# A deeper pipeline of attention jobs, a reordered second layer and whole-row norms in a three-part transformer kernel

## The reference

```python
def first_block(x, p, ...):                       # one layer
    proj = rmsnorm(x, attn_pre_g) @ w_in          # q, and keys and values of four kinds
    k_cmp, v_cmp = compress_kv(kc, ...), compress_kv(vc, ...)
    o_nsa = nsa_attention(q_n, k_cmp, v_cmp, ksl, vsl, kwn, vwn, gates, slopes)  # cmp + slc + win
    o_swa = swa_attention(q_s, k_s, v_s, sinks, slopes)                          # sliding, 128 wide
    x = x + rmsnorm(concat(o_nsa, o_swa) @ w_o, attn_post_g)
    y = gelu(causal_dwconv(a)) * u  @ w_down      # a, u = split(rmsnorm(x) @ w_gate_up)
    x = x + rmsnorm(y, mlp_post_g)
    return x + (p @ w_ple) * sigmoid(x @ w_ple_gate)

def hybrid_layer(x, ...):                         # twice, on 16 + 512 tokens
    q, k, v, gate_a, u_b, gate_b, q_idx, k_idx, w_idx, merge = split(rms_norm(x) @ w_in)
    # index scores choose for each query which keys it sees (the rest is masked), then attention
    y_a = (attention(rope(norm(q)), rope(norm(k)), v, chosen) * silu(gate_a)) @ w_a
    y_b = (multiscale_pool(u_b) * silu(gate_b)) @ w_b
    return x + (sigmoid(merge_a) * y_a + sigmoid(merge_b) * y_b) @ w_out
```

## Time and profile before

| | us |
|---|---|
| median of 3 runs | 1639.17 |
| lowest and highest | 1632.9 and 1644.02 |
| the profiled execution | 1644.22 |
| its span, first to last instruction | 1642.3 |
| PE busy in the span | 1547.3 |
| POOL, DVE, ACT busy | 972.7, 907.3, 542.9 |

### The profile page before, as it was taken

One profiled execution on the slowest core, in us unless ns is written; L12 is line 12 of the kernel. 1 busy time (PEld: TensorE's weight loads), 2 busy tenths in 40 slices (PEclk: granted clock), 3 DMA queues, 4 the chain that ended last, 5 costly groups with the idle time before them and its releaser, 6 DMA issues.

```text
span 1642.3 us, 26836 instructions
## 1 busy us (share of the span) xinstructions
PE 1547.3 (94%) x9758; PEld 1305.0 (79%) x9758; DVE 907.3 (55%) x2009; ACT 542.9 (33%) x1285; POOL 972.7 (59%) x1540
## 2 busy tenths in 40 slices
PE   6989878989999999998999999999999989899999
PEld 6766544757778777886899988889999977788999
DVE  4444555157667670017567778944446679684251
ACT  3244565233333320013365233341135523223210
POOL 5442400645655678778886655446888663255685
PEclk9999988989999999999999999999999998799999
DMA  6111000212223223332222212112222221111223
GB/s 234 52 52 39 27 1 1 65 51 90 89 89 102 90 89 103 97 95 65 85 76 78 78 52 65 52 52 72 91 91 77 74 70 41 38 63 55 72 94 106
DMA packets 37353, 119.59 MB, mean 73 GB/s; under 512 B 5376, under 2 KB 7552, under 8 KB 36992
## 3 DMA queue, kind: packets, MB, share of 16 engines
q1 hardware_dynamic: 35824, 115.74, 21.6%
q10 hardware_dynamic: 1424, 2.41, 0.4%
HBM read 116.02 MB, written 2.10 MB: 72 GB/s over the span
## 4 chain that ended last, share of the span: by engine, by line
PE 77%; DVE 12%; ACT 4%; issue 3%; POOL 3%; DMA 0%; ACTq 0%; POOLq 0%; SPq 0%; DVEq 0%
PE ps L682 62%; PE ps L701 2%; DVE score L2183 2%; PE ps L1123 2%; DVE score L2182 2%; PE ps L869 2%; POOL wlo L586 2%; PE ps L803 2%; PE ps L1199 1%; PE ps L695 1%; PE ps L714 1%; ACT pts L1399 1%; POOL whi L582 1%; DVE probs L2303 1%; DVE probs L2284 1%
## 5 line engine op out<-in xcount | busy, mean ns | idle before, releaser
L682 PE MATMUL ps<-hh,whi 128*128 128x512 f32 (+2 forms) x1736 | 572.0, 330 | 17.7 <-ACT merge L1643 6.2
L682 PE MATMUL ps<-hl,whi 128*128 128x512 f32 (+2 forms) x1736 | 560.9, 323 | 0.0
L682 PE MATMUL ps<-hh,wlo 128*128 128x512 f32 (+2 forms) x1736 | 559.8, 322 | 0.0
L582 POOL TENSOR_SCALAR whi<-raw 128x256 fp32r<-128x256 f32 x592 | 266.0, 475 | 380.2 <-PE ps L682 369.6
L586 POOL TENSOR_TENSOR wlo<-raw,whi 128x256 fp32r<-128x256 f32 x592 | 463.5, 813 | 12.3
L682 PEld LDWEIGHTS ps<-hh,whi 128*128 128x128 f32 x1736 | 331.0, 191 | 62.6 <-issue 20.2
L682 PEld LDWEIGHTS ps<-hh,wlo 128*128 128x128 f32 x1736 | 331.2, 191 | 25.4
L682 PEld LDWEIGHTS ps<-hl,whi 128*128 128x128 f32 x1736 | 331.0, 191 | 25.1 <-issue 2.0
L646 POOL TENSOR_TENSOR wlo<-raw,whi 128x256 fp32r<-128x256 f32 x160 | 134.8, 873 | 92.7 <-ACT whi L1442 92.7
L1791 DVE TENSOR_TENSOR tmp<-tmp 128x512 f32<-128x512 f32 x14 | 11.6, 826 | 134.7 <-ACT tmp L1481 101.1
L682 PE MATMUL ps<-plain_high,whi 128*128 128x264 f32 (+2 forms) x288 | 83.6, 290 | 1.9 <-POOL wlo L586 1.5
(11 more groups left out here) (315 smaller groups left out, 2721.2 us busy)
## 6 DMA issues: line engine op xcount, KB each, us to landing
raw<-in_w SPq DMA_DIRECT2D x200, 512.0 KB, 3.3
x<-in_x SPq DMA_DIRECT2D x4, 512.0 KB, 7.4
out<-x SPq DMA_DIRECT2D x8, 256.0 KB, 6.0
raw<-in_w SPq DMA_DIRECT2D x12, 128.0 KB, 2.6
raw<-in_w SPq DMA_DIRECT2D x4, 384.0 KB, 3.3
cw_k<-in_cw1k SPq DMA_DIRECT2D x1, 1024.0 KB, 5.5
cw_v<-in_cw1v SPq DMA_DIRECT2D x1, 1024.0 KB, 7.3
raw<-in_w SPq DMA_DIRECT2D x4, 256.0 KB, 2.9
```

The costliest lines, as they stand in the source:

```text
L582: ins = pool.tensor_scalar(whi[s][:, c:c + PIECE], raw[s][:, c:c + PIECE], 1.0, 0.0, ALU.mult, ALU.add)
L682: mm = pe.matmul(out, lhs, rhs, start=start and n == 0, stop=stop and n == 2)
```

## The change

- **Attention jobs.** Everything behind `biased` comes one round later: DVE does `weighted(i-2)`, PE transposes job i-3 and finishes job i-4, ACT copies job i-3 and puts only one exponential ahead of the copies. There are four buffers: the 8 sliding jobs share `probs` by halves of a row, the later ones use `third`, `probs` and the place of a weight tile that is no longer needed. A job waits for the transposes of the job four before it.
- **Fills.** `FIRST` has the window keys behind two query units of group 0, and `fills1` projects them in round 9 (from round 6). The queries of group 1 come in rounds 14 and 17 (from 10 and 13). SP's loads and POOL's splits follow `FIRST`.
- **"pre" norm.** DVE adds up the squares of the 8 chunks, and PE sums them in four matmuls at the end. ACT's first square waits for the transfer of `late` too.
- **Embedding.** `embed_out` 1 to 3 stand before ACT's loop, 4 to 7 in its first four rounds. The root of the tokens comes right behind `embed_out(0)`.
- **Start of both hybrid layers.** The inverse root is again a whole row of 528 on all partitions: 2 matmuls over the summed squares, a root on ACT, a reciprocal on DVE. The keys' norm waits for query unit 0 on PE, then takes 2 matmuls, a row-wide mean on DVE, root on ACT and reciprocal on DVE, and four multiplications. All of it stands ahead of the first rotation on DVE. The four sets of small matmuls (L737 twice, L1085, and the spreading of the keys' factor) and `keys_out` go.
- **Last layer's plan.** Two more merges are in the lead and the index scores of tile 2 stand closer together. All picks of tile 2 are at the end of DVE's lead, not in slots 0 and 1. Side work of tile 3 is in slots 0 to 4 (from 2 to 5), of tile 4 in slots 5 to 9 (from 6 to 9).

```diff
 FIRST = [U_VSL, U_VWN, U_VS, U_KS, U_Q + 4, U_Q + 5, U_Q + 6, U_Q + 7,
-         U_KC, U_VC, U_KSL, U_KWN, U_Q, U_Q + 1, U_Q + 2, U_Q + 3]
+         U_KC, U_VC, U_KSL, U_Q, U_Q + 1, U_KWN, U_Q + 2, U_Q + 3]
...
-        fills1 = {0: [6], 1: [7], 2: [8], 3: [9], 4: [10], 5: [11, "hk"], 6: [12, "hv"], 7: [13, "ck"],
-                  8: ["cv"], 10: [14], 13: [15]}
+        fills1 = {0: [6], 1: [7], 2: [8], 3: [9], 4: [10], 5: [11, "hk"], 6: ["hv"], 7: [12, "ck"],
+                  8: ["cv"], 9: [13], 14: [14], 17: [15]}
...
+        fourth = cw1["k"][:].rearrange("p c m -> p (c m)").rearrange("p (r t) -> p r t", r=REP)
+        SHORT = GROUPS * QT
         def probs1(n):
-            return third if n % 3 == 2 else probs[:, n % 3]
+            if n < SHORT:
+                return probs[:, n // 2 % 2, :, 2 * P * (n % 2):2 * P * (n % 2 + 1)]
+            return (third, fourth, probs[:, 0], probs[:, 1])[n % 4]
+        def last_user1(n):
+            return None if n < 4 or SHORT <= n < SHORT + 2 else {SHORT + 2: SHORT - 3, SHORT + 3: SHORT - 1}.get(n, n - 4)
         def stats1(n):
-            return small3 if n % 3 == 2 else small[:, 8 * (n % 3):8 * (n % 3) + 8, :]
+            return (small, small3)[n // 2 % 2][:, 8 * (n % 2):8 * (n % 2) + 8, :]
...
                 two, picks = side_steps(2)[0:HEADS // 2], side_steps(2)[HEADS // 2:]
-                ga, mg = named("ga0 ga1 ga2 ga3"), named("mg0 mg1")
-                lead = ga[0:2] + two[0:1] + ga[2:3] + score_first + ga[3:] + two[1:2] + mg[0:1] + two[2:3] + mg[1:] + two[3:]
-                lead_act = ga[0:2] + two[0:1] + ga[2:] + score_first + two[1:2] + mg[0:1] + two[2:3] + mg[1:] + two[3:]
-                lead_dve = rest + ga[0:2] + score_first + two[0:1] + ga[2:3] + [("weighted", 0)] + ga[3:] + two[1:]
-                side[0] += picks[0:4]
-                side[1] += picks[4:]
-                units = ["gb0", "ub0", "mg2", "gb1", "ub1", "mg3", "gb2 mg4", "ub2 mg5", "mg6", "gb3 mg7", "ub3", "mg8",
-                         "mg9 mg10", "mg11 mg12", "mg13", "mg14 mg15"]
+                ga, mg = named("ga0 ga1 ga2 ga3"), named("mg0 mg1 mg2 mg3")
+                indexed = two[1:3] + mg[0:1] + two[3:] + mg[1:]
+                lead = ga[0:2] + two[0:1] + ga[2:3] + score_first + ga[3:] + indexed
+                lead_act = ga[0:2] + two[0:1] + ga[2:] + score_first + indexed
+                lead_dve = rest + ga[0:2] + score_first + two[0:1] + ga[2:3] + [("weighted", 0)] + ga[3:] + two[1:] + picks
+                units = ["gb0", "ub0", "mg4", "gb1", "ub1", "mg5", "gb2 mg6", "ub2", "mg7", "gb3 mg8", "ub3", "mg9",
+                         "mg10", "mg11 mg12", "mg13", "mg14 mg15"]
                 mixed = {2: 0, 5: 1, 8: 2, 11: 3}
-                spans = [(3, 2, 6), (4, 6, 10)]
+                spans = [(3, 0, 5), (4, 5, 10)]
...
-            for k in range(DC):
-                pe.wait_ge(*at("squared", ("pre", k)))
-                token_sums("pre", tmp[:, k % 2, 0:S], [(X, G)[t // 2][:, t % 2, 0:1] for t in range(QT)],
-                           k == 0, k == DC - 1).then_inc(*tick("squares_summed", ("pre", k)))
+            sum_tokens("pre", rstd[:, 0:S])
             spread_root("pre")
...
-            for i in range(len(jobs1) + 2):
+            for i in range(len(jobs1) + 3):
                 if i < len(jobs1):
                     scores1(i)
-                if i >= 3:
-                    weigh1(last_turn1[i - 3])
+                if i >= 4:
+                    weigh1(last_turn1[i - 4])
                 for f in fills1.get(i, ()):
                     fill1(f)
-                if i >= 2:
-                    n = i - 2
+                if i >= 3:
+                    n = i - 3
                     first = last_turn1[n - 1] + 1 if n else 0
                     for turn in range(first, last_turn1[n] + 1):
                         transpose1(turn)
...
-                        if (m, k) == (L_V, 2):
-                            pe.wait_ge(*at("token_rstd", tag))
-                            spread_halves(r_tok).then_inc(*tick("rstd_spread", tag))
...
-                pe.wait_ge(*at("squares_added", (tag, DC - 1)))
+                sum_added(tag, [X[:, 0, 0:TH], X[:, 1, 0:TH]], [total[:, 0:TH], total[:, TH:T]])
                 for j in range(QT + 1):
                     t0 = rows2(j)[0]
                     mm = pe.matmul(X[:, 0, 300 + j:301 + j], total[:, t0:t0 + P], ones[:, 0:1], start=True, stop=True)
                 mm.then_inc(*tick("tokens_summed", l))
                 whole(L_V, S0, 72)
-                pe.wait_ge(*at("k_raw", l))
-                pe.wait_ge(*at("layer_rstd", tag))
-                for j in range(QT + 1):
-                    t0 = rows2(j)[0]
-                    mm = pe.matmul(X[:, 0, 310 + j:311 + j], probs2[:, 0, t0:t0 + P], bones[:, 0:1], start=True, stop=True)
-                mm.then_inc(*tick("k_squares", l))
-                qunit(0, G)
+                qunit(0, G, at("k_raw", l))
+                pe.wait_ge(*at("rms_tok", l))
+                plain(X, bones, probs2[:, 0, :]).then_inc(*tick("k_squares", l))
...
                     qunit(c, (G, S1)[c % 2], at("q_raw", (l, c - 2)) if c >= 2 else None)
                     if c == 1:
-                        pe.wait_ge(*at("k_token", l))
-                        spread_halves(k_tok[2]).then_inc(*tick("k_spread", l))
...
+            act.wait_ge(*at("eps_in", 0))
             square_all("pre", lambda k: x[:, k, META:T], lambda k: at(f"x_in{k // 2}", 0), lambda k: tmp[:, k % 2, 0:S])
-            act.wait_ge(*at("eps_in", 0))
-            token_root("pre", [(small[:, 12, 0:2], X[:, :, 0]), (small[:, 12, 2:4], G[:, :, 0])])
+            token_root("pre")
...
-            for i in range(len(jobs1) + 3):
+            for i in range(len(jobs1) + 4):
                 exps = REP if 1 <= i <= len(jobs1) else 0
-                first = REP if i in fills1 else 2
+                first = REP if i in fills1 else 1
                 for r in range(min(first, exps)):
                     exped1(i - 1, r)
-                if i >= 3:
-                    mix_out(i - 3)
+                if i >= 4:
+                    mix_out(i - 4)
                 for f in fills1.get(i, ()):
                     fill1(f)
-                blocks = len(blocks1(jobs1[i - 2][0], jobs1[i - 2][2])) if 2 <= i < len(jobs1) + 2 else 0
+                blocks = len(blocks1(jobs1[i - 3][0], jobs1[i - 3][2])) if 3 <= i < len(jobs1) + 3 else 0
                 for b in range(max(blocks, exps - first)):
                     if b < blocks:
-                        turned_out(i - 2, b)
+                        turned_out(i - 3, b)
                     if first + b < exps:
                         exped1(i - 1, first + b)
...
             embed_out(0)
-            embed_out(1)
-            token_root("mpost", [(small[:, 12, 0:QT], X[:, 0, 0:QT])])
-            for m in range(2, 6):
+            token_root("mpost")
+            for m in range(1, 4):
                 embed_out(m)
             for k in range(DC):
...
-                if k < 2:
-                    embed_out(6 + k)
+                if k < 4:
+                    embed_out(4 + k)
...
                 act.wait_ge(*at("tokens_summed", l))
+                root(tag, halves(score[:, 0, :]), full(X), 1.0 / D)
...
                 act.copy(halves(value_rows()), full(S0)[0:72]).then_inc(*tick("v_rows", l))
                 act.wait_ge(*at("k_mean", l))
-                act.activation(k_tok[1], k_tok[0], ACT.Sqrt).then_inc(*tick("k_rms", l))
+                act.activation(score[:, 0, :], score[:, 1, :], ACT.Sqrt).then_inc(*tick("k_rms", l))
...
+            for k in range(DC):
+                add_square("pre", k, rstd[:, 0:S], tmp[:, k % 2, 0:S])
...
-                    dve.wait_ge(*at("turned", last_turn1[n - 3]))
+                if last_user1(n) is not None:
+                    dve.wait_ge(*at("turned", last_turn1[last_user1(n)]))
...
-            for i in range(len(jobs1) + 1):
+            for i in range(len(jobs1) + 2):
                 if i < len(jobs1):
                     biased(i)
-                if i >= 1:
-                    weighted(i - 1)
+                if i >= 2:
+                    weighted(i - 2)
...
-                dve.wait_ge(*at("rms_tok", l))
-                dve.reciprocal(r_tok, rms_tok).then_inc(*tick("token_rstd", tag))
-                dve.wait_ge(*at("token_rstd", tag))
-                dve.scalar_tensor_tensor(out=eps_tok, in0=rms_tok, scalar=EPS, in1=rms_tok, op0=ALU.mult, op1=ALU.mult)
-                dve.scalar_tensor_tensor(out=index_tok, in0=r_tok, scalar=(8 ** -0.5) * (HD ** -0.5), in1=r_tok,
-                                         op0=ALU.mult, op1=ALU.mult).then_inc(*tick("tokens", l))
+                dve.wait_ge(*at("rms", tag))
+                dve.scalar_tensor_tensor(out=score[:, 1, :], in0=score[:, 0, :], scalar=EPS, in1=score[:, 0, :],
+                                         op0=ALU.mult, op1=ALU.mult)
```

(41 more changed lines are left out.)

63 lines of the change are left out of this document (22 added, 41 removed).

## The result

The changed kernel takes 1595.75 us in the median of 4 runs (1593.41 to 1596.14), the kernel before 1636.91 beside it (1632.9 to 1644.02). The ratio is 0.9741, with a 95% interval of 0.9704 to 0.9778: faster by 2.6%, where 1596 was forecast. The profiled execution of the changed kernel has a span of 1593.8 us, 48.5 under that of before, whose profiled execution (1644.22 us) was slower than its median by 7.3 us, against 0.1 here. The two traces thus differ by 48.5 us, the two medians by 41.2.

The account below looks back on a forecast made before the run. PE, busy 1547.3 us, was taken as the bound, losing time to waits and lowered clock. The terms −26, +0.8, −2, −14 and −2.4 sum to −43.6, so 1600.6 beside 1644.22; 0.3% below gives 1596, range 1578 to 1622.

Parts of the forecast that it names:

- A: Attention jobs: deeper pipeline and moved fills, −16 us for waits, −1.5 for fills, −8.5 for clock; −26, from −10 to −33.
- The term for the clock: Attention jobs: PE's work returns to the full clock, 8.5 us taken of at most 11.8.
- Rival (2): Attention jobs: ACT sets the pace, gain only 10 us, 1612 in all; sign a wait on L1399 above 12; chance 0.12.
- B: First norm: DVE adds the squares, so PE's first sums end at 22.4 and not 21.58; +0.8 us.
- C: Start of both hybrid layers: row-wide norms, PE loses small matmuls, DVE's first low part comes later; −2 us, −4 to +4.
- the 1 us set aside for a lost clock: Start of both hybrid layers: 1 us given back because PE stands still longer and may lose clock.
- D: Last layer's plan: idle time of PE −9.5 us, clock −4.5; −14 in all, bounds −5 and −20.
- The stop that was named as left, ub1's: Last layer: PE's idle time falls to about 7 us, part of it for `ub1`, whose ACT part waits for a branch.
- E: Embedding: two copies fewer ahead of the first high part end DVE's wait and shrink PE's; −2.4 us, −1 to −3.
- Rivals (3): Last layer: the plan only moves waits from slots to the lead, gain 0 there, 1610 in all; chance 0.13.
- (4): Attention jobs and last layer: more comes than forecast, −33 and −20 us, 1583 in all; chance 0.04.

Follow-up runs that it names:

- a_noplan: The changed kernel with the last layer's plan as before; 1609.32 us, ratio to the kernel before 0.9801.
- a_nofills: The changed kernel with the old order of fills (window keys in round 6, group 1 queries in rounds 10 and 13); 1596.47 us, ratio to before 0.9736.
- a_noE: The changed kernel with the embedding's copies ahead of the loop again (6, not 4); 1597.59 us, ratio to before 0.9727.
- a_swap: The changed kernel with two units of the last layer's slot 9 exchanged (mg8, then gb3); 1591.35 us, ratio to before 0.9688.
- a_warm: The changed kernel with 10, 12 and 28 extra identity transposes on PE ahead of three remaining stops; 1589.73 us, ratio to before 0.9684.

## Why the prediction came out right, by its steps

**A, −26: right in sum, its shares off.** The jobs ended 26.2 us sooner and both parts taken back cost 27.2 us. The waits for `weighted` went as forecast (19.1 to 2.7). But waits as a whole fell by 12.4, not by 17.5. ACT's copies grew by 4.0 us, within what was left for them and for the window keys. Against it stand some 3.5 us for `weighted` that remain on all lines, the new 2.5 for `seg_k` and `seg_v`, and the fills of the compressed keys and values, which save 2.4 us together where 3.7 were put. The prediction read only two rows of PE's waits and not the 7.6 us for ACT's copies that were there already. Its bounds don't add up either: the terms' own give −8 to −34.9, not −10 to −33. The term for the clock made good for it, 12.5 where 8.5 was taken and 11.8 was called the most. That bound came from the granted clock of the last two stretches alone; the busy times of all the jobs (197.1 and 184.5) show that earlier ones had some of it too. Rival (2), ACT as the pace, did not decide: its wait of 11.6 us is near the mark of 12 set for it, yet 7.6 of that is old, each of the usual stops is 0.24 us, and ten of them between 194 and 261 us leave the clock at 0.97 to 1.00.

**B, +0.8: right in sum (+0.6) by two errors.** Timelines of the start after the change, PE, DVE and ACT (against the earlier trace rows):

```profile
21.82 1.83 PE L724 MATMUL ps<-const,rstd 128*128 128x1 f32 x8 [21.82 <-DVE rstd L1777]
...
14.86 6.82 DVE L1777 TENSOR_TENSOR rstd<-rstd,tmp 128x512 f32<-128x512 f32 x7
...
20.16 1.28 ACT L1291 ACT_TABLE_LOAD   x1
23.70 0.26 ACT L1291 ACTIVATE small<-ps,late 128x4 f32<-128x4 f32 x1 [2.26 <-PE ps L724]
```

Seven sums took 6.82 us, not 5.9. They don't wait for ACT, whose squares wait for them (0.17 to 0.50 us each); three took 0.70 us and four 1.03, and why the later ones are slower stays open. PE's sums end at 23.65, not at 22.4. The root behind them is shorter by 1.5 us. ACT loads the table for it at 20.16, while it waits; before, the load stood behind the last sum, at 21.65. I had not seen that step.

**C, −2: the mechanism right, the size low.** In DVE's timeline of layer 0 (against the earlier trace rows):

```profile
795.30 3.45 DVE L2124 RECIPROCAL score<-score 128x528 f32<-128x528 f32 x1 [0.34 <-ACT score L1559]
...
803.41 1.24 DVE L2100 TENSOR_TENSOR hl<-probs,hh 128x528 fp32r<-128x528 f32 x1
...
821.64 1.13 DVE L2188 TENSOR_TENSOR qi<-probs 128x528 f32<-128x528 f32 x1
```

The first low part is 4.0 us later in step (22.09 under 825.5, where the start of the stage is 26.05 under), and the fourth rotation 1.6 earlier (822.77 for 850.38), both as worked out. The stages are 1.4 and 2.8 shorter, and the 1 us set aside for a lost clock was not needed: the clock did fall for 3.4 us at 817.0, but the stage is 46.9 us with that and 46.8 without it in a_noplan. PE does stand still, but in layer 0 for POOL's splits alone (2.8 us in two stops) and in layer 1 for them (3.1) and 1.34 us for the rotation, where it was 1.7 in each before. POOL's splits were not in the prediction's account of C.

**D, −14: right in kind, some 3 low for the profiled execution.** Idle time fell by 11.5 (9.5 forecast) and busy time by 6.6 (4.5); in medians it is 13.6. But the account ran through relu, and PE's waits for relu were small before and after. What went is the stop behind DVE's picks (5.4), most of those for DVE's `score` (2.7) and 2.6 us of those for a place that ACT holds; the picks' move, which the prediction prices only through DVE, is thus the larger part. The stop that was named as left, ub1's, was not there; the same cause stood one part later, at gb3.

**E, −2.4: wrong.** The step that failed is "with two copies fewer ahead of it DVE's wait goes, and PE's shrinks by as much". PE's wait did shrink, by 2.6, but what came second was not looked up: POOL's splits. The prediction's own rule, to say what is late next, was not kept for this term. Rivals (3) and (4) fell with the sizes of D and A.

The terms' errors don't cancel in the traces: there C and D brought 2.2 and 4.1 us more than forecast and E 2.8 less, and with the small rest it is −48.5 for a forecast of −43.6. In medians it is −41.2 for −43. The forecast lies between the two, and that 1596 meets 1595.75 to within 0.3 us is luck, given how the kernel before scatters.

## What to carry to other kernels

Price a stop of PE by its length and by what runs behind it: here some 19 of 48.5 us were matmuls that no longer ran at the lower clock, mostly behind stops of 2 to 4 us, which cost it often but not each time. Where a stop can't be removed, fill it with matmuls that nobody reads, into a place that PE itself overwrites next. And for each wait that a change takes away, look for the one that ends next behind it on another engine: the embedding's 2.4 us went to POOL, and the wait for gb3's place was left standing, where the exchange of two units gave 4.4 us more.

## What the runs showed of the hardware

- Extra transposes of the identity, 8 to 16 ahead of each of eight stops, held the granted clock at 1.00 where it was 0.81 and 0.85.
- Behind one and the same stop of 2.90 to 3.11 us the next 48 matmuls took 7.31 to 8.46 us in eight executions and 5.94 in one. Behind a stop of 2.18 us four products took 1.12 us in the changed kernel and 0.65 in a_nofills, a_noE, a_swap and a_warm. Behind one of 4.30 us the first matmuls ran at 0.63 us each, not 0.40.
- Stops of 0.24 us, ten of them between 194 and 261 us, left the clock at 0.97 to 1.00. But in the changed kernel the clock also fell for 6.8 us at 1318.8, where the stops just ahead were of 0.57 us and less, and it didn't fall behind one of 1.88 us at 1227.51.
- The last layer's slots took 172.4 us in a_nofills, 174.7 in a_noE and 176.7 to 177.0 in seven others, the changed kernel among them, all with the same code there. Where the clock falls seems in part to be chance from one execution to the next; what decides it stays open.
